# Moving one gate group of layer 1's modulation tiles from layer 0's output stage to the stretch between the layers

## The reference, cut to what matters

```python
sh, sc, gt = modulation(c, ada_w[l], ada_b[l])
h = rms_norm(x, norm_pre[l]) * (1.0 + sc[:, None]) + sh[:, None]
z = h @ w_in[l]
# attention, Hyena convolution and gMLP branches out of z, merged to out
out = merge_branches(z, (y_a, y_b, y_c), w_branch[l], w_out[l])
x_new = x + gt[:, None] * rms_norm(out, norm_post[l])
```

## Time and profile before

| what | value |
|---|---|
| median of three runs | 1434.15 us |
| the profiled execution, its own time | 1432.28 us |
| its span | 1431.0 us |
| outside the span | 1.28 us |
| mean granted TensorE clock | 0.987 of full speed |
| TensorE busy | 1374.4 us (96%) |
| VectorE busy | 936.4 us (65%) |
| ScalarE busy | 686.8 us (48%) |
| bytes moved | 202.21 MB, mean 141 GB/s |

### The profile page before, as it was taken

One profiled execution on the slowest core, in us unless ns is written; L12 is line 12 of the kernel. 1 busy time (PEld: TensorE's weight loads), 2 busy tenths in 40 slices (PEclk: granted clock), 3 DMA queues, 4 the chain that ended last, 5 costly groups with the idle time before them and its releaser, 6 DMA issues.

```text
span 1431.0 us, 20879 instructions
## 1 busy us (share of the span) xinstructions
PE 1374.4 (96%) x8316; PEld 1162.7 (81%) x8316; DVE 936.4 (65%) x1688; ACT 686.8 (48%) x1190; POOL 41.6 (3%) x50
## 2 busy tenths in 40 slices
PE   6999999999999999989999999988999999999998
PEld 3676677778888887669789899987889989888878
DVE  6564664876333434398876787657877777888556
ACT  5434554134322232545455454455556746666445
POOL 0000000000000000200000000010000002000001
PEclk9999999999999999999999999998999999999999
DMA  9431351254322233513234455544543345555552
GB/s 366 169 103 59 139 197 48 71 176 144 103 90 101 91 106 104 193 59 104 88 119 133 155 174 191 180 163 137 191 133 119 104 149 175 192 191 192 198 170 74
DMA packets 57937, 202.21 MB, mean 141 GB/s; under 512 B 6288, under 2 KB 9680, under 8 KB 57840
## 3 DMA queue, kind: packets, MB, share of 16 engines
q1 hardware_dynamic: 55712, 194.27, 40.1%
q0 software_dynamic: 1760, 6.12, 1.3%
q10 hardware_dynamic: 368, 0.48, 0.1%
HBM read 199.80 MB, written 1.05 MB: 140 GB/s over the span
## 4 chain that ended last, share of the span: by engine, by line
PE 83%; DVE 10%; ACT 3%; DMA 2%; issue 1%; SPq 0%; DVEq 0%; ACTq 0%
PE gemm_bank L417 16%; PE gemm_bank L418 15%; PE gemm_bank L419 15%; PE misc_bank L417 4%; PE misc_bank L418 4%; PE misc_bank L419 4%; PE misc_bank L428 3%; PE gemm_bank L428 3%; DVE wlo L1711 2%; PE gemm_bank L573 1%; PE misc_bank L429 1%; PE gemm_bank L429 1%; PE misc_bank L573 1%; PE misc_bank L857 1%; PE gemm_bank L506 1%; PE misc_bank L816 1%
## 5 line engine op out<-in xcount | busy, mean ns | idle before, releaser
L1711 DVE TENSOR_TENSOR wlo<-raw,whi 128x1024 fp32r<-128x1024 f32 x316 | 383.1, 1223 | 74.6 <-ACT whi L1194 71.2
L1194 ACT ACTIVATE whi<-raw 128x1024 fp32r<-128x1024 f32 x316 | 332.6, 1055 | 163.3 <-PE gemm_bank L419 95.9
L417 PE MATMUL gemm_bank<-halves,wlo 128*128 128x256 f32 (+1 forms) x1152 | 376.4, 327 | 16.9 <-DVE halves L2244 4.2
L418 PE MATMUL gemm_bank<-halves,whi 128*128 128x256 f32 (+1 forms) x1152 | 361.4, 314 | 0.0
L419 PE MATMUL gemm_bank<-halves,whi 128*128 128x256 f32 (+1 forms) x1152 | 361.1, 313 | 0.0
L417 PEld LDWEIGHTS gemm_bank<-halves,wlo 128*128 128x128 f32 x1152 | 223.5, 194 | 40.6 <-issue 17.3
L419 PEld LDWEIGHTS gemm_bank<-halves,whi 128*128 128x128 f32 x1152 | 223.9, 194 | 12.0
L418 PEld LDWEIGHTS gemm_bank<-halves,whi 128*128 128x128 f32 x1152 | 224.2, 195 | 11.1 <-issue 0.7
L417 PE MATMUL gemm_bank<-arena_r,wlo 128*128 128x512 f32 (+1 forms) x320 | 108.4, 339 | 0.9 <-DVE wlo L1711 0.9
L419 PE MATMUL gemm_bank<-arena_r,whi 128*128 128x512 f32 (+1 forms) x320 | 107.8, 337 | 0.0
L418 PE MATMUL gemm_bank<-arena_r,whi 128*128 128x512 f32 (+1 forms) x320 | 107.8, 337 | 0.0
(11 more groups left out here) (417 smaller groups left out, 2261.5 us busy)
## 6 DMA issues: line engine op xcount, KB each, us to landing
raw<-in_stream SPq DMA_DIRECT2D x348, 512.0 KB, 3.3
arena<-in_stream SPq DMA_DIRECT2D x16, 512.0 KB, 12.6
x<-in_x SPq DMA_DIRECT2D x1, 1024.0 KB, 6.5
x<-in_ctx SPq DMA_DIRECT2D x1, 1024.0 KB, 9.4
y<-in_hy_decay POOLq DMA_DIRECT2D x2, 512.0 KB, 4.2
arena<-in_gm_ws POOLq DMA_DIRECT2D x2, 512.0 KB, 6.5
const_b<-in_const_b POOLq DMA_DIRECT2D x1, 635.0 KB, 6.3
y<-in_hy_w POOLq DMA_DIRECT2D x2, 256.0 KB, 3.7
```

The costliest lines, as they stand in the source:

```text
L417: mm(out, w_lo, r_hi, start=first, stop=False)
L418: mm(out, w_hi, r_lo, start=False, stop=False)
L1194: act.activation(self.whi[:, t % SPLIT, :], self.raw_tile(t), ACT.Copy).then_inc(*self.mark("tile_hi", "tile_hi", t))
L1711: dve.tensor_tensor(self.wlo[:, t % SPLIT, :], self.raw_tile(t), self.whi[:, t % SPLIT, :].bitcast(F32), ALU.subtract).then_inc(*self.mark ...
```

## The change

Group 4 of layer 1 leaves the output stage of layer 0. Its four tiles now stand between the query tiles and the key tiles of layer 1 in the list. TensorE, however, takes them before the query tiles: behind the eight sums of squares of side 0 and ahead of the first query product, which needs the new rows. Group 5 stays in the output stage, its two pairs now behind o = 2 and o = 3, and is turned at o = 4. ScalarE copies group 4's sums out of PSUM after the fourth piece of side 0's rows (`act_beside`), TensorE turns them behind the last key tile, and VectorE adds them up and finishes both gate groups between the second and the third part of the rotation. The PSUM bank of the group is the one ahead of the first query's; the turned sums go to misc bank 0, so that the first scores of layer 1 wait for VectorE to have read them. ScalarE's split of a key tile waits for the query tile whose buffer it takes, eight places earlier in the list instead of four.

```diff
-WOUT_ADA = {0: (4, (0, 1)), 1: (4, (2, 3)), 3: (5, (0, 1)), 4: (5, (2, 3))}
+CROSS_ADA, WOUT_ADA = (1, 4), {2: (5, (0, 1)), 3: (5, (2, 3))}
@@ plan
+        if l:
+            cross_use, uses = uses, uses + 1
         for kind in ("q", "k") if l else ("k", "q"):
             for j in range(4):
                 add(kind, l, j, n if kind == "q" else ALL, 1)
+            if l and kind == "q":
+                for q in range(4):
+                    add("ada", 1, (CROSS_ADA[1], q), 0, 0)
+                    tiles[-1].use = cross_use
@@ pe_cross
+        queries, moving, keys = (self.tiles[self.pe_next + 4 * i:self.pe_next + 4 * i + 4] for i in range(3))
         for k in range(KT):
             self.pe_cross_sum(0, k)
+        for T in moving:
+            self.pe_tile(T)
         self.pe_cross_queries(queries)
         for i, side in CROSS_KEYS:
             self.pe_cross_keys(keys[i], side, (i, side) == (0, 1))
-        self.pe_next += 8
+        self.pe_turn(*CROSS_ADA)
+        self.pe_next += 12
@@ pe_attention
+        if l:
+            pe.wait_ge(*self.at("turned", *CROSS_ADA))
@@ pe_block1 (and dve_block1 with dve_turned)
-            if l == 0 and o in (2, 5):
-                self.pe_turn(1, 4 + o // 3)
+            if l == 0 and o == 4:
+                self.pe_turn(1, 5)
@@ act_hi
-                act.wait_ge(*self.at("used", t - SPLIT))
+                held = t - SPLIT
+                while held > FRONT + SPLIT and self.tiles[held].kind == "ada":
+                    held -= SPLIT
+                act.wait_ge(*self.at("used", held))
@@ act_beside, new
+    def act_beside(self, l, g):
+        T = next(T for T in self.tiles if T.kind == "ada" and T.l == l and T.j == (g, 3))
+        self.act.wait_ge(*self.at("used", T.t))
+        self.act.wait_ge(*self.at("ada_turn", l, 5))
+        m = self.act.activation(self.rows(l, g), self.ada_bank(T)[:, :], ACT.Copy)
+        m.then_inc(*self.mark("act_evac", "evac", T.use))
+        self.also("rows", l, g)
@@ act_cross_h
+            if s == 0 and k == 3:
+                self.act_beside(*CROSS_ADA)
@@ dve_cross
-        for _ in range(4):
+        for _ in range(8):
             self.dve_lo()
@@ dve_block1
         for r, (a, b) in enumerate(ROPE):
             self.dve_rope(l, a, b)
+            if l and a == 3:
+                self.dve_turned(*CROSS_ADA)
+                self.dve_mod_gate(1)
...
-                self.dve_mod_gate(1)
```

More of the change, by code:

```diff
@@ L224 @@
     FRONT_GROUPS = tuple((0, g) for g in FRONT_ADA)
+    BESIDE = (CROSS_ADA,)
     LATE_ADA = ((0, 4), (0, 5), (1, 0), (1, 1))
@@ L593, in pe_turn @@
                 pe.wait_ge(*self.at("turned", *ASIDE[0]))
+        elif (l, g) in self.BESIDE:
+            b = self.turn_bank(l, g)
+            if (l, g) == CROSS_ADA:
+                pe.wait_ge(*self.at("root", ("res", 0), 1))
         else:
@@ L599, in pe_turn, with turn_bank @@
         m.then_inc(*self.mark("pe_turn", "ada_turn", l, g))
+    def turn_bank(self, l, g):
+        return self.M[3] if (l, g) in ASIDE else self.M[0] if (l, g) == CROSS_ADA else self.M[3]
     def ada_bank(self, T):
@@ L784, in pe_cross @@
     def pe_cross(self):
-        queries, keys = self.tiles[self.pe_next:self.pe_next + 4], self.tiles[self.pe_next + 4:self.pe_next + 8]
+        queries, moving, keys = (self.tiles[self.pe_next + 4 * i:self.pe_next + 4 * i + 4] for i in range(3))
         for k in range(KT):
             self.pe_cross_sum(0, k)
+        for T in moving:
+            self.pe_tile(T)
         self.pe_cross_queries(queries)
@@ L1208, in act_tile @@
             g, q = j
-            if q == 3:
+            if q == 3 and (l, g) not in self.BESIDE:
                 act.wait_ge(*self.at("used", T.t))
@@ L1213, in act_tile @@
                 elif T.t >= FRONT:
-                    act.wait_ge(*self.at("ada_turn", l if g else 0, g - 1 if g else 5))
+                    act.wait_ge(*self.at("ada_turn", l if g else 0, (3 if (l, g) == (1, 5) else g - 1) if g else 5))
                 elif g != FRONT_ADA[0]:
@@ L1513, in act_cross @@
         self.act_tap_root(1)
-        self.act_hi()
+        for _ in range(5):
+            self.act_hi()
         for k in range(KT):
@@ L1526, in act_cross @@
             self.act_tiles(1)
+        self.act_tiles(4, split=False)
         act.wait_ge(*self.at("summed", ("res", 0, 1), KT - 1))
@@ L1833, in dve_turned @@
         aside = (l, g) in ASIDE
-        bank = self.M[3] if aside else self.G[self.extra["ada", l, g] % 4]
+        aside = aside or (l, g) in self.BESIDE
+        bank = self.turn_bank(l, g) if aside else self.G[self.extra["ada", l, g] % 4]
         self.dve.wait_ge(*self.at("ada_turn", l, g))
@@ L2157, in dve_mod_gate @@
         v, mod, b = self.dve, self.mods[l], self.both(f"ada_b{l}", 24)
-        v.wait_ge(*self.at("evac", self.extra["ada", l, 5]))
+        if l:
+            v.wait_ge(*self.at("turned", *CROSS_ADA))
+            v.wait_ge(*self.at("evac", self.extra["ada", l, 5]))
+        else:
+            v.wait_ge(*self.at("evac", self.extra["ada", l, 5]))
         self.own(v.tensor_tensor(mod[:, 16:24, :], mod[:, 16:24, :], b[:, 16:24, :], ALU.add))
@@ L2267, in dve_block1 @@
         if l:
-            self.dve_tiles(6, split=False)
+            self.dve_tiles(10, split=False)
             self.dve_tiles(2)
@@ L2298, in dve_block1 @@
                 self.dve_hidden(1, o // 2)
-            if l == 0 and o in (2, 5):
-                self.dve_turned(1, 4 + o // 3)
+            if l == 0 and o == 4:
+                self.dve_turned(1, 5)
             if l == 0 and o == 5:
@@ L2650, in _layout @@
             tiles.append(_columns(w[:, c:c + 512]))
+            if l and c:
+                ada(1, CROSS_ADA[1], CROSS_ADA[1] + 1)
         tiles.append(_rows(w[:, 512:1024]))
@@ L2681, in _layout @@
             at = len(tiles)
-            ada(1, 4, 6)
+            ada(1, 5, 6)
             both, done = tiles.pop(at), 0
```

## The result

| | time, us (lowest to highest, runs) | profiled execution / span, us |
|---|---|---|
| before | 1434.05 (1432.19 to 1439.18, 20) | 1432.28 / 1431.0 |
| changed | 1438.51 (1433.77 to 1442.79, 20) | 1436.60 / 1435.3 |

The ratio is 1.0027, 95% interval 1.0017 to 1.0037: by it the changed kernel is slower by 3.9 us, between 2.4 and 5.3; the two medians lie 4.5 us apart. The forecast was 1437.7.

What follows compares the result with a forecast made beforehand. TensorE, busy 96% of the span, was taken as the bound, VectorE at layer 1's start. Terms -3.6 + 7.2 - 0.5 + 0.4 = +3.5 us on 1434.15 gave 1437.65, rounded 1437.7; range 1432.0 to 1440.5, own case 1436.0 to 1439.8.

Steps and rivals of the forecast that it cites:

- The output stage, -3.6 us: Output stage of layer 0: two ada pairs 2.27, one group's transposes 0.45 and a 0.91 us wait go, 3.6 us earlier.
- turns up there: Output stage: if the low-half wait stays or appears at the fifth output tile, the gain is only 2.7 us.
- the slack of 0.4 us: Output stage, fifth output tile: about 7.2 us available for load, split and subtraction that took 6.8 us.
- The fourth tile's load: Between the layers: fourth ada load goes out at 631.55 after VectorE's low half, lands 3.9 us later (3.1 to 4.5).
- the first rival: Load landing of 4.5 us, output-stage wait moved, 24 slow products: +5.5 us, 1439.7 us; chance 0.16.
- The fourth tile's own length: Between the layers: the fourth ada tile, half of a pair, takes 0.5 us at full clock, 1.05 us at 1.2 GHz.
- The clock, -0.5 us: First query products of layer 1: about 19 slow instead of 24, 0.5 us back, bounds 0 to 1.2 us.
- 0.50 for about 5 us: Sign to check: TensorE's granted clock stays at 0.50 for about 5 us once work begins again between the layers.
- ScalarE and VectorE between the layers: Between the layers: ScalarE's copy and VectorE's low halves resume at about 637.1, end near 641; the delay is hidden.
- VectorE in the rotation, +0.4 us: Rotation before layer 1's first scores: one reduction and two gate instructions add 0.4 us, bounds 0 to 0.6.
- The third: Rival: landing of 3.1 us and a warm clock behind the first scores, +0.95 us, 1435.1 us; chance 0.14.
- The second: Rival: fourth ada load goes out before side 0's rows and doesn't hold TensorE, -3.7 us, 1430.4 us; chance 0.10.

Runs made afterwards that it cites:

- the pairs stay at the front: The changed kernel with group 5's two pairs behind o = 0 and 1 of the output stage instead of o = 2 and 3: 1440.16 us, ratio 1.0045.
- the low half at piece 0: The changed kernel with the fourth query tile's low half formed at k = 0 of side 0's rows instead of k = 3: 1437.81 us, ratio 1.0025.
- the gate behind the scores: The changed kernel with the reduction and two gate instructions moved from the rotation to behind the first maxima: 1436.38 us, ratio 1.0008.
- the kernel that meets its condition: The changed kernel with the fourth query tile's low half swapped with side 1's reciprocal, so formed before side 0's rows: 1431.09 us, ratio 0.9975.
- both kernels that had no other delay: Kernel before plus 9 idle products ahead of the queries: 1432.98 us; changed kernel with early low half, late gate steps, six idle products before scores: 1429.67 us.

## Why the prediction was right

**The output stage, -3.6 us.** Measured -3.66. The wait of 0.91 us for the third output tile's low half is gone in the changed kernel and comes back, with 1.18 us, when the pairs stay at the front. In the changed kernel's two profiles no other tile is late. But with the low half at piece 0 the fifth tile was, by 0.40 us, as in the bound "turns up there": the slack of 0.4 us held by luck as much as by reckoning.

**The fourth tile's load.** The load went out at 631.8 (631.55 foretold), right behind a low half of VectorE, and TensorE showed one wait of 7.9 us ahead of a single ada tile (about 8 foretold). It landed in 3.3 us where I took 3.9, inside the bounds of the earlier trace rows; that term was 0.6 us too large. No kernel here showed the 4.5 us of the first rival for this load.

**The fourth tile's own length.** This term was too small: 1.92 us, not 1.05. I had halved the pair's 1.06 us. But where the low half comes early, the same single tile takes 1.05 us at full clock: alone it costs as much as a pair does. The two errors nearly cancel, which is luck: the first query came 7.43 us later against "open", where the sum had 7.2.

**The clock, -0.5 us.** The sum had 19 products at 1.2 GHz. The six profiles with this long wait show 6, 8, 9, 17, 18 and 18, against 23 before. The rise came 3.3 us after work began again in the changed kernel, 3.7 in its second profile, 5.8 with the pairs at the front and 6.0 with the gate behind the scores: a wider spread than the 3.5 to 5.15 us with which I had bounded it. From the first query to side 1's reciprocal it took 19.52 us before and 17.82 in the changed kernel, so there the term is worth 1.7 us, beyond the 1.2 of my bound; it is 1.5 in the second profile and down to 0.5 in the others. The sign "0.50 for about 5 us" failed in both profiles of the changed kernel.

**ScalarE and VectorE between the layers: hidden.** VectorE stood 4.82 us at 638.20 for ScalarE's pieces behind the copy, and TensorE waited for none of them: no such wait is in its list.

**VectorE in the rotation, +0.4 us.** Measured +0.6 (gap 46.95 against 46.34, and 46.36 once the instructions are out): it was the end at which each result is awaited.

**The sum.** In the profile the terms make -3.66 + 7.43 - 1.70 + 0.61 = +2.7 us, and would make some +3.8 with 18 slow products; the scores are 3.04 us later because 0.36 came in ahead of the stage. The forecast was +3.5, the measured ratio says +2.4 to +5.3. So the mechanism was right, and that the number came so near owes something to errors that went both ways. What stays open is how soon the clock comes back in most runs, and with it up to a microsecond of the median. The low end of the prediction's own range is added up wrongly: -0.8 - 0.1 - 0.7 - 0.4 from +3.5 is +1.5 us, not +1.8. The first rival, with all its bad ends, didn't come: the landing was short and the stage's wait gone. The third asked for a landing of 3.1 us and a warm clock behind the scores. The first profile had 1.2 GHz there, the second had the clock up although TensorE had waited 3.57 us in both. So its condition on the clock holds in some executions and not in others, where the prediction took it as fixed; what it is worth in the median no run here shows.

The second, where the load goes out before the rows, was priced at 1430.4 us; the kernel that meets its condition ran in 1431.09. Its terms fit too: -3.66, -0.55 and +0.60 us against -3.6, -0.5 and +0.4. But what takes most of the warm clock's gain back there is the third piece of the rows, behind the moved reciprocal, and not the first sum of side 1.

## What to carry to other kernels

When a piece of work is moved into a hole of the bounding engine, ask first when its input can be there: in a ring of buffers filled in order, a tile inherits the release of the tile that had its buffer before, and one late release holds everything queued behind it. Look whether the call that makes this release can be moved as well; here that one swap turned 1438.35 us into 1431.09. Filling a rest to keep the clock up gave back less than its slow products in both kernels that had no other delay (1.1 of 2.3 us, 0.7 of 1.75), because the next engine down the line was the one waited for then.

## What the runs showed of the hardware that I had not expected

- **Half a pair saves nothing.** An ada tile's two products go to two of the bank's four strips of 32 partitions (`pe_tile`). A pair, which fills all four (x8 records), takes 1.06 us, a single tile (x4) 1.05 us, three (x12) 1.91 us: the second tile of a pair runs beside the first.
- **Neither the return nor the fall of the clock is fixed.** After rests of 7.7 to 8.0 us the rise to 2.4 GHz took 3.3, 3.7, 5.8 and 6.0 us of work in four executions, after 5.9 us it took 4.0, after 9.3 us 5.7. After one and the same wait of 3.57 us ahead of the scores the clock was at 1.2 GHz in one execution of the changed kernel (0.51 in 703.50 to 706.90) and at full in the other. The Trainium skill, page "TensorE: Matmul & The Clock Gate", section "What's actually happening", has activity release the throttle and calls the number of slow products run-variable; the traces agree, with 6 and 8 of them in the changed kernel's two profiles.
- **The spread goes with the clock.** Over the 20 runs of the changed kernel the time goes with the mean granted clock: 1433.77 us at 0.991, 1442.79 us at 0.979. Two profiles of the same kernel spent some 44 and 27 us at 1.2 GHz (added up from the granted clock in stretches of 1 us) and differ by 2.9 us in span. That the clock causes the spread no experiment here shows. So a local gain of under a microsecond shows in the distances of a trace, and not in a median of ten runs.
